# Rotary embedding by ScalarE's copies instead of TensorE's turning matmuls

## The reference

```python
ROT_DIM = HEAD_DIM // 4            # 32 of 128 channels are rotated
def partial_rope(x, positions):
    inv_freq = ROPE_THETA ** (-jnp.arange(0, ROT_DIM, 2) / ROT_DIM)
    ang = positions[..., None] * inv_freq
    cos, sin = jnp.cos(ang)[:, :, None, :], jnp.sin(ang)[:, :, None, :]
    xr = x[..., :ROT_DIM]
    x1, x2 = xr[..., :ROT_DIM // 2], xr[..., ROT_DIM // 2:]
    rot = jnp.concatenate([x1 * cos - x2 * sin, x2 * cos + x1 * sin], axis=-1)
    return jnp.concatenate([rot, x[..., ROT_DIM:]], axis=-1)

for gi, (window, dilation) in enumerate(((128, 1), (512, 4), (2048, 16))):
    q = partial_rope(heads(bq), positions); k = partial_rope(heads(bk), positions)
    o, lse = dilated_window_attention(q, k, v, dilation, window // (2 * dilation))
# the three branches are joined by a softmax over their log denominators,
# then: mixed = concat(delta, dilated);  out = mixed @ w_out
```

## Time and profile before

| | us |
|---|---|
| median of 3 runs | 3708.77 (3701.34 to 3710.35) |
| the profiled execution | 3710.74 |
| its span | 3708.9 |
| TensorE busy | 3520.8 (95%) |
| VectorE busy | 2241.4 (60%) |
| ScalarE busy | 1547.8 (42%) |
| the dilated stage in it | about 738 to 1101 |

### The profile page before, as it was taken

One profiled execution on the slowest core, in us unless ns is written; L12 is line 12 of the kernel. 1 busy time (PEld: TensorE's weight loads), 2 busy tenths in 40 slices (PEclk: granted clock), 3 DMA queues, 4 the chain that ended last, 5 costly groups with the idle time before them and its releaser, 6 DMA issues.

```text
span 3708.9 us, 80229 instructions
## 1 busy us (share of the span) xinstructions
PE 3520.8 (95%) x35884; PEld 3177.7 (86%) x35884; DVE 2241.4 (60%) x3391; ACT 1547.8 (42%) x2400; POOL 251.7 (7%) x302
## 2 busy tenths in 40 slices
PE   8899989999979999999999999999999999999988
PEld 8888989888868888888888888988888888888877
DVE  8666765555655888885545445355565655556555
ACT  5333333333334444444434444333554444444333
POOL 0021011000000000000001010001201101011000
PEclk9999989999989999999999999999999999999999
DMA  5433543565435555555554333434433333333254
GB/s 203 180 130 146 186 170 121 197 259 191 150 114 174 174 190 183 189 185 194 173 179 149 111 135 131 148 128 165 151 111 107 115 111 112 112 117 113 102 210 148
DMA packets 94391, 571.47 MB, mean 154 GB/s; under 512 B 12688, under 2 KB 20912, under 8 KB 32096
## 3 DMA queue, kind: packets, MB, share of 16 engines
q1 hardware_dynamic: 80496, 511.85, 39.4%
q0 software_dynamic: 13552, 54.49, 4.4%
HBM read 536.01 MB, written 30.28 MB: 153 GB/s over the span
## 4 chain that ended last, share of the span: by engine, by line
PE 81%; DVE 10%; ACT 5%; DMA 2%; issue 2%; POOL 0%; SPq 0%; DVEq 0%; ACTq 0%; POOLq 0%
PE banks L286 17%; PE banks L287 8%; PE banks L2099 4%; PE banks L308 3%; PE banks L309 3%; PE banks L310 3%; PE banks L1039 3%; PE banks L273 3%; PE banks L1040 3%; PE banks L1041 3%; PE banks L2100 3%; PE banks L2101 3%; PE banks L274 3%; PE banks L275 3%; PE banks L2296 2%
## 5 line engine op out<-in xcount | busy, mean ns | idle before, releaser
L253 DVE TENSOR_TENSOR w_lo<-ring,w_hi 128x2048 fp32r<-128x2048 f32 x274 | 629.3, 2297 | 452.9 <-ACT w_hi L247 452.9
L247 ACT CAST w_hi<-ring 128x2048 fp32r<-128x2048 f32 x274 | 522.5, 1907 | 252.4 <-PE banks L287 111.3
L286 PE MATMUL banks<-x_two,w_hi 128*128 128x512 f32 x1408 | 499.0, 400 | 0.3 <-PE banks L1125 0.3
L287 PE MATMUL banks<-x_two,w_lo 128*128 128x256 f32 x1408 | 396.0, 281 | 0.0
L2155 DVE TENSOR_TENSOR w_lo<-ring,w_hi 128x512 fp32r<-128x512 f32 x316 | 217.3, 689 | 246.3 <-ACT w_hi L2112 245.2
L1039 PE MATMUL banks<-x_two,w_hi 128*128 128x256 f32 x1152 | 350.3, 304 | 7.2 <-DVE w_lo L1106 7.2
L1040 PE MATMUL banks<-x_two,w_hi 128*128 128x256 f32 x1152 | 332.3, 288 | 0.0
L1041 PE MATMUL banks<-x_two,w_lo 128*128 128x256 f32 x1152 | 331.6, 288 | 0.0
L2099 PE MATMUL banks<-XK,w_hi 128*128 128x256 f32 x1024 | 316.9, 310 | 11.3 <-DVE w_lo L2155 11.3
L286 PEld LDWEIGHTS banks<-x_two,w_hi 128*128 128x128 f32 x1408 | 265.3, 188 | 66.9 <-issue 0.7
L2100 PE MATMUL banks<-XK,w_hi 128*128 128x256 f32 x1024 | 290.3, 283 | 0.0
(11 more groups left out here) (540 smaller groups left out, 8318.5 us busy)
## 6 DMA issues: line engine op xcount, KB each, us to landing
ring<-in_w_up SPq DMA_DIRECT2D x88, 1024.0 KB, 4.9
ring<-in_w_dil SPq DMA_DIRECT2D x72, 1024.0 KB, 5.0
mod_ring<-in_w_mod SPq DMA_DIRECT2D x48, 1024.0 KB, 7.3
ring<-in_w_logit SPq DMA_DIRECT2D x48, 1024.0 KB, 5.1
ring<-in_w_down SPq DMA_DIRECT2D x44, 1024.0 KB, 4.9
ring<-in_w_delta SPq DMA_DIRECT2D x32, 1024.0 KB, 5.0
ring<-in_w_out SPq DMA_DIRECT2D x32, 1024.0 KB, 4.9
ring<-in_w_na SPq DMA_DIRECT2D x32, 1024.0 KB, 4.8
```

The source lines that it names most:

```text
L247: nc.scalar.copy(w_hi[:, s, 0:w], ring[:, s, 0:w]).then_inc(S("panel_hi"), 4)
L253: nc.vector.tensor_tensor(w_lo[:, s, 0:w], ring[:, s, 0:w], w_hi[:, s, 0:w].bitcast(F32), ALU.subtract).then_inc(S("panel_split"), 1)
L286: nc.tensor.matmul(out_ap, hi, both, start=first_, stop=False)
L287: return nc.tensor.matmul(out_ap[:, 0, :], lo, both[:, 0, :], start=False, stop=last_)
```

## The change

The rotated channels are reordered on the host in the q and k panels of `w_dil`, so that the first half lies on partitions 0 to 15 and the second on 32 to 47 (16 to 31 and 48 to 63 carry channels that are not rotated; their frequency is 0, so their sine is 0 and their cosine 1). The exchange of halves is then a copy of 32 partitions to another 32, which ScalarE does in two copies to a head (`swap`), of 32 x 1536 each, into `rot`. `rot` is now 64 partitions by all six tiles and lies over `Sc`, which is free once P is transposed. VectorE rotates in three operations of 64 x 1536, with the sign in `sinb`. Swap and rotation of head h + 1 stand in head h: ScalarE's copies behind the copies of P, with two steps between them and four after; VectorE's between steps 15 and 16. For head 0 they stand ahead of the loop, for head 7 in its beginning. The turning matmuls and the constant are gone, and TensorE's waits for `dil_out` and `vtok_ready` move to where the banks are now written. The first whole split (tiles 0 to 7) moves from head 7 to the end of head 3, on VectorE ahead of the copy of the mixed head; TensorE's output tiles 0 to 7 move ahead of head 7's scores.

```diff
-            if h:
-                pe.wait_ge(S("dil_out"), h)
-                pe.wait_ge(S("vtok_ready"), h)
-            for b in range(NBR):
-                last = nc.tensor.matmul(banks[3 + b][0:64, :], C("turn", 0, 64)[0:32, :], QK[u][0:32, 2 * b:2 * b + 2, :],
-                                        start=True, stop=True)
-            last.then_inc(S("turned"), 1)
+            if h == LAST:
+                pe.wait_ge(S("whole_ready"), 1)
+                wout_tiles(pe, 0, 8)
             F(4)
             pe.wait_ge(S("roped"), h + 1)
...
             if h == LAST:
                 pe.wait_ge(S("whole_ready"), 2)
-                wout_tiles(pe, 0, 14)
+                wout_tiles(pe, 8, 14)
...
+        def swap(h, half):
+            if half == 0 and h < LAST:
+                act.wait_ge(S(f"dil_loaded{h % 2}"), 32 * (h // 2 + 1))
+            r = slice(32 * half, 32 * half + 32)
+            q = slice(32 - 32 * half, 64 - 32 * half)
+            nc.scalar.copy(rot[r, :, :], QK[h % 2][q, :, :]).then_inc(S("qk_swapped"), 1)
+
+        swap(0, 0)
+        swap(0, 1)
         for h in range(HEADS):
             if h == LAST:
                 for _ in fill:
                     pass
-                whole_act(act, 0)
+                act.wait_ge(S("ev_ready"), 9 * HEADS)
+                swap(h, 0)
+                swap(h, 1)
                 act.wait_ge(S("dil_out"), LAST - 1)
                 whole_act(act, 1)
...
                 nc.scalar.copy(PT[:, 4:6, q * P:(q + 1) * P], b4(1)[:, 2 * q:2 * q + 2, :]).then_inc(S("pt_ready"), 1)
-            F(6)
+            if h + 1 < LAST:
+                swap(h + 1, 0)
+                F(2)
+                swap(h + 1, 1)
+                F(4)
+            if h == 3:
+                whole_act(act, 0)
...
+        def rope(h):
+            qk = QK[h % 2][0:64, :, :]
+            dve.wait_ge(S("qk_swapped"), 2 * h + 2)
+            nc.vector.tensor_tensor(qk, qk, six(cosb[:, :]), ALU.mult)
+            ch(nc.vector.tensor_tensor(rot[:, :, :], rot[:, :, :], six(sinb[:, :]), ALU.mult))
+            nc.vector.tensor_tensor(qk, qk, rot[:, :, :], ALU.add).then_inc(S("roped"), 1)
...
-            if h == LAST:
-                whole_dve(dve, 0)
+                rope(h)
             F(4)
...
-            F(6)
+            F(4)
+            if h + 1 < LAST:
+                rope(h + 1)
+            F(2)
+            if h == 3:
+                whole_dve(dve, 0)
             dve.wait_ge(S("dil_mixed"), h + 1)
```

More of the change, by code:

```diff
@@ L87, in constants @@
     c["merge"] = np.concatenate([same(2 * n) & ~same(n) for n in (8, 16, 32)], 1)
[L88 to L92, removed]
     start = np.ones((P, P))
@@ L97, in constants @@
     f = np.zeros((P, 1), np.float32)
-    f[:32, 0] = np.concatenate([inv, inv])
+    f[0:16, 0] = inv
+    f[32:48, 0] = inv
     c["freq"] = f
+    c["sign"] = np.where(s < 32, -1.0, 1.0)
     c["eps"] = np.full((P, 1), EPS)
@@ L924, in program @@
     PT = place("PT", D0 + 33, [P, NBR * TT, T])
[L925 to L933, removed]
+    cosb = place("cosb", D0 + 39, [64, T])
+    sinb = place("sinb", D0 + 40, [64, T])
+    rot = place("rot", D0 + 27, [64, 2 * NBR, T])
+    cos0 = place("cos0", 116, [64, T])
+    sin0 = place("sin0", 117, [64, T])
+    pos_i = place("pos_i", 118, [64, T], I32)
+    pos_n = place("pos_n", 121, [64, T], I32)
+    ang = place("ang", 122, [64, T])
+    nf = place("nf", 123, [64, T])
     amax, arec, asum = stat[:, 0:4], stat[:, 4:8], stat[:, 8:12]
@@ L941, in angles_dve @@
         yield
-        ch(nc.vector.tensor_scalar(ang[:, :], ang[:, :], one("freq")[0:32, :], None, ALU.mult))
+        ch(nc.vector.tensor_scalar(ang[:, :], ang[:, :], one("freq")[0:64, :], None, ALU.mult))
         yield
@@ L1166, in dil_pe @@
             last.then_inc(S("scored"), 1)
+            if h:
+                pe.wait_ge(S("vtok_ready"), h)
             for b in range(NBR):
@@ L1184, in dil_pe @@
             pe.wait_ge(S("vtok_ready"), h + 1)
+            if h:
+                pe.wait_ge(S("dil_out"), h)
             for m in range(2 * NBR):
@@ L1237, in dil_dve @@
         nc.vector.tensor_copy(RS[1][:, :], RS[0][:, :])
-        ch(nc.vector.tensor_copy(sinb[:, :], sin0[:, :]))
-        wide = lambda ap: ap.rearrange("p (a t) -> p a t", a=1).to_broadcast([32, 2, T])
+        ch(nc.vector.tensor_scalar(sinb[:, :], sin0[:, :], one("sign")[0:64, :], None, ALU.mult))
+        six = lambda ap: ap.rearrange("p (a t) -> p a t", a=1).to_broadcast([64, 2 * NBR, T])
+        def rope(h):
[4 more added lines that the diff above has]
+            nc.vector.tensor_tensor(qk, qk, rot[:, :, :], ALU.add).then_inc(S("roped"), 1)
+        rope(0)
         for h in range(HEADS):
@@ L3192, in host_arrays @@
     o["w_delta"] = np.concatenate([q[k * 8 + h * 4:k * 8 + h * 4 + 4] for h in range(2) for k in range(4)])
-    q = panels(w[:, 4 * W + 32:]).reshape(3, NBR, HEADS, P, D)
+    q = w[:, 4 * W + 32:].reshape(D, 3, NBR * HEADS, P).copy()
+    order = np.concatenate([np.arange(16), np.arange(32, 48), np.arange(16, 32), np.arange(48, P)])
+    q[:, 0:2] = q[:, 0:2][..., order]
+    q = panels(q.reshape(D, -1)).reshape(3, NBR, HEADS, P, D)
     o["w_dil"] = q.transpose(2, 1, 0, 3, 4).reshape(HEADS * 9, P, D)
@@ L3202, in host_arrays @@
     o["mask3"] = dilated_masks()
-    o["pos"] = np.broadcast_to(i["positions"].reshape(1, T).astype(np.int32), (32, T))
+    o["pos"] = np.broadcast_to(i["positions"].reshape(1, T).astype(np.int32), (64, T))
     cw = i["conv_qkv_w"][0].T.reshape(3, 2, 4, P, 5).transpose(3, 1, 0, 2, 4).reshape(P, 120)
```

## The result

| | before | changed |
|---|---|---|
| median of 20 runs each, us | 3711.17 (3699.56 to 3715.11) | 3718.56 (3708.47 to 3724.53) |
| ratio to before, 95% interval | | 1.0023 (1.0014 to 1.0031) |
| the profiled execution, us (its span) | 3710.74 (3708.9) | 3712.68 (3710.8) |
| TensorE busy, us | 3520.8 | 3500.0 |
| ScalarE busy, us | 1547.8 | 1572.3 |

The change makes the kernel slower by 0.23%, some 8 us, with 20.8 us less of busy TensorE. The predicted time was 3703, with a range up to 3713. The measured 3718.56 lies outside.

A forecast was written before the change was run, and what follows sets the result against it. TensorE was taken as the bound (81% of the last-ending chain), almost balanced with its helper chain at step 16. Terms -5.6 - 2.2 + 3.3 + 1.3 + 4.4 - 7.6 = -6.4 us gave 3704.3, forecast 3703, range 3689 to 3713.

The forecast's parts named there:

- what would show it: Signs in the dilated stage: no turning matmuls, copies at 1.48 us, named TensorE waits, clock 0.5 after the two longest.
- Step 16 and the heads 1 to 3: Filler steps are numbered 0 to 19 per head; TensorE enters 16 1.37 us later, heads 1 to 3 still gain.
- rival C: Clock falls behind every hole of 2 us, up to four more falls: +7 us, 3710; chance 0.10.
- Entering head 4: The first whole split delays VectorE's low halves; TensorE idles 5.2 us: +3.3 us, plus 2.2 for half clock.
- Entering head 6: ScalarE waits for V's load before the swap; TensorE idles 5.7 us: +1.3 us, plus 2.2 for half clock.
- The last head: 16 of 28 output tiles fill the hole before the scores, which may run at faster clock: -7.6 us.
- Rival D: The last head gains nothing because VectorE's chain sets its end: 3710; chance 0.05.
- Head 0: Removing the turn is worth nothing here: TensorE waits another 1.79 us for modulation weights anyway.
- Rival A: Swaps cost TensorE nothing and V's load lands in time: -25 us, 3684; chance 0.20, including something half way.
- The rule on the clock: Half clock follows the two long pauses, entering heads 4 and 6: 2.2 us each, +4.4, between 0 and 7.
- The forecast's last step: From the profiled execution's 3704.3 to the runs' median, 2.0 us lower: predicted 3703.

The follow-up runs named there:

- e0_again: The changed kernel itself, unchanged, run for a second trace: 1.0017 of the kernel before, 3714.54 us.
- e2_split: The changed kernel with the first whole split moved from behind head 3's last filler step into gaps of head 3: 1.000 of before, 0.9983 of the changed kernel.
- e1_layout: The kernel before with only the change's data side (reordered channels, 64-partition tables and positions), the turn still on TensorE: 0.9995 of before.
- e5_before_pad: The kernel before plus 40 one-column matmuls in the last head's wait for the rotation: 1.0015 of before.
- e3_gaps: The changed kernel with swap, rotation and first whole split all moved into gaps, `rot` in its own memory: 0.9953 of before, 3688.25 us.
- e6_gaps_pad: The kernel of e3_gaps plus 24 one-column padding matmuls in front of head 0: 0.9914 of before, 3678.17 us.
- e0b_again: The changed kernel unchanged once more, beside the padded one on the same chip: 1.0025 of before.
- e7_swap: The changed kernel with only the swaps of heads 1 to 5 moved before the wait for P's transposes, `rot` in its own memory: 0.9964 of before.
- e4_pad: The changed kernel plus 24 one-column padding matmuls in front of head 0: 0.9975 of before, 3701.62 us.
- e4b_pad: The changed kernel with the 24 padding matmuls of e4_pad, measured once more: 0.998 of before.

## Why the prediction was wrong

**The scan, outside every term of the sum.** The changed kernel loses 8.5, 8.6 and 9.5 us from 2800 us on in its three traces. The forecast had nothing there: I had summed only what the change touches. The step that failed is the unspoken one that removed instructions cost only their own time: they also move the points at which TensorE waits for its next instructions, 8.2 to 9.4 us of such waits in the scan instead of 2.3. No rival named it, and none of the signs listed under what would show it looks behind the stage. The same kernel with padding measured 0.9975 and 0.998, so 3702 us by either median, where the forecast was 3703; but that it comes so near is in part luck, since the scan accounts for only half of what the padding gained, and the terms within the stage missed in both directions.

**Step 16 and the heads 1 to 3.** The forecast had TensorE enter step 16 1.37 us later; the wait grew by 1.64 in heads 0 to 4 (0.46 to 2.10 and 0.68 to 2.32). What I left to rival C, a fall of the clock behind holes of 2 us, came true: 0.57 in the rows at 787 and 924, where steps 16 and 17 start 24 matmuls over 4.2 us instead of 2.9. So heads 1 to 3 gained 1.4 us together where 6.7 were forecast, the largest miss within the sum. From scores to scores the heads took, mean of the changed kernel's three traces against the one of before, and what was forecast:

```
into head            1      2      3      4      5      6     scores of 7 to last tile
before             49.4   48.3   45.8   41.5   41.5   42.6   32.6
changed, mean      48.3   47.5   46.3   46.8   41.1   43.3   25.7
difference         -1.1   -0.8   +0.5   +5.3   -0.4   +0.7   -6.9
forecast           -2.8   -2.8   -1.1   +5.5   -1.1   +3.5   -7.6
```

**Entering head 4** was right in mechanism, and in size with the clock: +5.3 against +5.5. The parts differ: the wait was 3.73 us where an idle stretch of 5.2 was worked out, because TensorE came to it later, its steps 16 and 17 having run at half clock. In `e0b_again`, where the clock did not fall at that step 16, the wait was 5.14 us. `e2_split` shows the hole and the clock behind it as caused by the split.

**Entering head 6**: the wait for V's load was real but short. The load landed in 7.0 us instead of 8.6, ScalarE waited 1.80 us instead of 3.4, and TensorE 4.09 instead of 5.7. +0.7 us on average instead of +3.5. (The prediction's own rows give 5.45 us for that wait, 0.68 + 1.37 + 3.4, not 5.7.) The half clock that was taken as gone from the kernel before comes and goes with the execution: `e1_layout` and `e5_before_pad`, which keep the turn, have none there and take 41.5 us into head 6, not 42.6.

**The last head** gave 6.9 of 7.6 us. The 16 output tiles run in the hole, the scores started 0.05 us sooner (counted from the scores of head 6), and the scores ran at 4.0 us instead of 5.3, part of the 0 to 2.6 that were open. Rival D is out.

**Head 0** gave nothing, as forecast. **Rival A** did not happen at the place given, but `e3_gaps` and `e6_gaps_pad` show it as true of the idea: 27 and 32 us off the stage, where A said 25. The rotation without TensorE is worth that; where the change puts its helpers, 3 us of it remain (363.0, 360.2 and 362.6 against 365.1), and even these are not clear of the spread, since the stage with the turn took 364.1 us in `e1_layout` and 361.9 in `e5_before_pad`.

**The sum.** Stage -3.2 us on the mean of three traces (forecast -6.4), scan +8.9: +5.7, which lies in the intervals of all three measurements (1.0023, 1.0017, 1.0025: +6 to +9 us). The forecast's last step has a slip: 3704.3 less 2.0 is 3702.3, not 3703.

**The rule on the clock.** "TensorE: Matmul & The Clock Gate" of the Trainium skill, in "Why this matters for your kernels", warns of long idle gaps between bursts of matmuls. The traces agree for the two long holes (0.60 at 938, 0.50 at 1013), and go further: holes of 2.1 and 2.3 us were followed by 0.57 at 787 and 924. Of the five such holes in the first trace (786.7, 835.0, 883.5, 924.3 and 970.8) four were followed by slow steps, the one at 883.5 was not; in the other two traces of the changed kernel it was five of five (`e0_again`) and two of five (`e0b_again`).

## What to carry to other kernels

A helper's work is free only in a stretch where its engine waits for the engine that bounds the kernel; here 1.5 us of ScalarE between two casts cost 2.8 to 3.2 us a head (changed kernel against `e7_swap`, heads 1, 2, 3 and 5) of the 3.3 that the turn is worth, and the same copies a few positions earlier cost nothing. So before moving work to a half-idle engine, read its timeline for waits on the bounding engine, and put each piece there. And when a change shortens or lengthens the program of the bounding engine, compare the traces far behind the change as well: if issue waits come and go in untouched code, count the instructions ahead of them, and let a padding test separate them from the change's own worth.

## What the runs showed of the hardware that was not expected

**Waits for the next 256 instructions.** 2.3 us of issue waits in the scan with the old count of TensorE's instructions (2.6 in `e1_layout`), 8.2 to 9.4 with 96 fewer (8.2 to 11.2 with `e2_split`, `e3_gaps` and `e7_swap`, whose TensorE program is the same), 9.8 with 160 more at the same instructions, 3.7 with 48 fewer, 1.5 to 2.7 with 96 fewer and 96 put back. All stand at one place in each 256 instructions, as counted above, and the instruction queue's traffic (283 packets, 4.64 MB) is 16 KB a packet. In the 4 us in which the changed kernel has its 2.49 us wait, the queues moved:

```profile
q0 software_dynamic: 309, 0.76, 64.9%
q1 hardware_dynamic: 173, 0.37, 24.1%
q8 instruction: 1, 0.02, 1.5%
```

One instruction packet lies there, beside 0.76 MB of loads in small packets. It took 0.97 us, as the others do (median 1.00), so it was late because it started late: at 3413.28, when TensorE's wait began. In the 2 us before their packet started, the 16 DMA engines were at least 90% busy for 60 of the 80 waits, and for 297 of the 1289 places of the same kind in the scans (2800 to 3500 us) at which TensorE did not wait. That a burst of loads delays the packet's start fits this; it is not shown, since no run changed the loads.

**Two paces of the same matmuls.** Between 1200 and 1700 us an execution either matches the trace of the kernel before within 1.5 us (seven of the twelve other traces) or gains 7.9 to 9.4 us on it (five), in code that no run touches. TensorE's timeline at 1300 us, the kernel before and then the changed one:

```profile
1299.89 0.40 PE L286 MATMUL banks<-x_two,w_hi 128*128 128x512 f32 x1
...
1302.72 0.40 PE L286 MATMUL banks<-x_two,w_hi 128*128 128x512 f32 x1
```

```profile
1299.91 0.39 PE L283 MATMUL banks<-x_two,w_hi 128*128 128x512 f32 x1
...
1302.68 0.39 PE L283 MATMUL banks<-x_two,w_hi 128*128 128x512 f32 x1
```

Eight pairs take 2.83 us or 2.77, at a granted clock of 1.00 in both. The changed kernel has one trace at the fast pace and two at the slow one, so one program can run at either. It is a good part of the 15 us over which runs of one kernel spread, and a reason why a difference of 0.2% needs many of them. Where six runs came out better than the traces allow (`e4_pad`, `e6_gaps_pad`, `e7_swap`), more executions at the fast pace could be the cause; with one trace to a run that is not shown, and `e4b_pad` kept most of its surplus over twelve runs. What sets the pace stays open.
